# A diffusion backbone kernel: filler matmuls ahead of attention, late modulation columns moved to the first MLP, semaphore clears inside other stages

## What is computed

```python
for i in range(2):
    mod_l = silu(c) @ mod_w[i] + mod_b[i]
    sh_a, sc_a, gt_a, sh_m, sc_m, gt_m = split(mod_l, 6)
    hl = rms_norm(xl, norm_g[i, 0]) * (1 + sc_a) + sh_a
    yl = ab_mixer(hl, hc, ...) if i == 0 else conv_mixer(hl, ...)
    xl = xl + gt_a * rms_norm(yl, norm_g[i, 1])
    hm = rms_norm(xl, norm_g[i, 2]) * (1 + sc_m) + sh_m
    xl = xl + gt_m * rms_norm(square(relu(hm @ w1[i])) @ w2[i], norm_g[i, 3])
```

```python
s_loc = einsum('bqhgd,bkhd->bhgqk', qblk, kb) * scale      # 3 blocks of 128 keys, banded
s_ctx = einsum('bqhgd,bkhd->bhgqk', qblk, kc) * scale      # 256 context keys
p = softmax(concatenate([s_loc, s_ctx, s_sink], axis=-1))
out = p[..., :n_loc] @ vb + p[..., n_loc:n_loc + L] @ vc
```

## Time and profile before

| | us |
|---|---|
| median of three runs | 1872.45 |
| lowest and highest of them | 1869.65, 1876.17 |
| the profiled execution | 1864.61 |
| its span, first to last instruction | 1862.4 |
| TensorE busy | 1681.7 (90%) |
| VectorE, ScalarE, GpSimd busy | 721.1, 571.2, 860.4 |

### The profile page before, as it was taken

The page is one execution under the profiler, slowest core; times in us unless marked ns, Lnnn a source line. Parts: engine busy times, 40 slices in busy tenths (PEclk is TensorE's granted clock), DMA queues, the critical chain, the costliest instruction groups (busy, mean ns, idle before and its releaser), DMA issues. The chain is left out here.

```text
span 1862.4 us, 35642 instructions
## 1 busy us (share of the span) xinstructions
PE 1681.7 (90%) x15570; PEld 1379.0 (74%) x15570; DVE 721.1 (39%) x1060; ACT 571.2 (31%) x816; POOL 860.4 (46%) x399
## 2 busy tenths in 40 slices
PE   4899999976788889588999999999998999999996
PEld 2688778865667678366788888888886778888885
DVE  2332233337757675554212121461066431212134
ACT  3423233343343432223313232313222242313230
POOL 1433100008786763243687888763443244444441
PEclk9998955558999999787999999978998799999998
DMA  8211100002231222211344334421221112222221
GB/s 327 106 68 68 32 1 1 1 0 71 71 137 50 93 72 72 75 68 45 136 142 152 135 135 152 147 71 45 105 90 68 68 59 101 90 92 111 90 90 45
DMA packets 23618, 162.16 MB, mean 87 GB/s; under 512 B 2624, under 2 KB 3264, under 8 KB 4800
## 3 DMA queue, kind: packets, MB, share of 16 engines
q1 hardware_dynamic: 21904, 154.09, 23.1%
q10 hardware_dynamic: 1584, 6.13, 0.8%
HBM read 157.71 MB, written 2.10 MB: 86 GB/s over the span
## 5 line engine op out<-in xcount | busy, mean ns | idle before, releaser
L218 POOL TENSOR_TENSOR v<-raw,v 128x1024 fp32r<-128x1024 f32 x160 | 387.8, 2445 | 427.1 <-ACT v L206 401.0
L235 PE MATMUL bank<-hm,v 128*128 128x512 f32 x2112 | 487.5, 392 | 10.4 <-PEq L161 4.6
L235 PEld LDWEIGHTS bank<-hm,v 128*128 128x128 f32 x2112 | 398.5, 189 | 100.2 <-issue 12.7
L235 PE MATMUL bank<-hid,v 128*128 128x512 f32 x1536 | 349.5, 389 | 0.0
L235 PEld LDWEIGHTS bank<-hid,v 128*128 128x128 f32 x1536 | 288.4, 188 | 59.8
L206 ACT ACTIVATE v<-raw 128x2048 fp32r<-128x2048 f32 x77 | 147.5, 1916 | 421.0 <-PE bank L235 420.9
L1975 DVE TENSOR_TENSOR bank<-bank,rl 128x512 f32<-128x512 f32 x64 | 44.7, 699 | 277.4 <-ACT rl L1954 277.4
L218 POOL TENSOR_TENSOR w<-raw,w 128x1024 fp32r<-128x1024 f32 x22 | 54.1, 2481 | 137.2 <-ACT w L206 137.2
L949 POOL TENSOR_TENSOR kt<-kt,kk 128x768 f32<-128x768 f32 (+2 forms) x12 | 14.9, 1270 | 216.6 <-ACT kt L1263 216.6
L935 POOL TENSOR_TENSOR raw<-raw,cs 128x2048 f32<-128x2048 f32 x24 | 87.0, 3627 | 51.1 <-DVE at L1380 51.1
L512 PE MATMUL bank<-h,w 128*128 128x512 f32 x600 | 108.8, 343 | 0.0
(11 more groups left out here) (286 smaller groups left out, 2413.1 us busy)
## 6 DMA issues: line engine op xcount, KB each, us to landing
raw<-w_in SPq DMA_DIRECT2D x119, 1024.0 KB, 4.8
mraw<-wm_in SPq DMA_DIRECT2D x16, 1024.0 KB, 4.8
raw<-wm_in SPq DMA_DIRECT2D x3, 1024.0 KB, 15.8
xres<-x_in ACTq DMA_DIRECT2D x1, 2048.0 KB, 8.3
yb<-wm_in SPq DMA_DIRECT2D x2, 1024.0 KB, 19.2
mixed_in<-wm_in SPq DMA_DIRECT2D x2, 1024.0 KB, 23.1
xres<-x_in SPq DMA_DIRECT2D x1, 2048.0 KB, 7.3
out_T<-xres ACTq DMA_DIRECT2D x8, 256.0 KB, 2.0
```

The lines of the kernel that those rows point to most:

```text
L218: i = nc.gpsimd.tensor_tensor(W[1][n % 2][:, k:k + 4], raw[n % 2][:, k:k + 4], W[0][n % 2][:, k:k + 4].bitcast(F32), SUB)
L235: last = nc.tensor.matmul(bank(b(s, m), 0, hi - lo), W[w][s][:, k, m * P:(m + 1) * P], H[h][:, k, lo:hi], start=(k == 0 and w == h == 0), ...
```

## The change

It has three parts.

1. Four fillers stand behind the scores of units 0 and 1, and two ahead of each of units 1 and 2.
2. Twenty of the late columns stand at the end of the first MLP, behind a wait for `mprod_free` and ahead of `over_channels`. Twelve stay in the late norm: four in place of its first filler, six behind the first broadcast (`over_partitions`, L185), two behind the second. None stands between the token sums.
3. `clear` and `clear_then_block` are gone. Semaphores live longer: those of the first stages until the end of the RWKV stage, the RWKV stage's own until the end of the first MLP, all others to the program's end. `reset` clears the first list (59) on GpSimd at the start of the RWKV stage, and the second (47) on GpSimd at the start of the first MLP. The 66 others aren't cleared.

```diff
+    until_rwkv, until_mlp = ExitStack(), ExitStack()
+    signals = {until_rwkv: [], until_mlp: [], top: []}
+
     def sems(stack, *names):
-        return [stack.enter_context(nc.semaphore(own(n))) for n in names]
+
+        out = [stack.enter_context(nc.semaphore(own(n))) for n in names]
+        signals[stack] += out
+        return out
+
+    def reset(pool, stack):
+
+        for s in signals[stack]:
+            pool.sem_clear(s)
...
-    def clear(stack_sems):
-
-        with nc.Block() as block:
-            @block.gpsimd
-            def _(pool):
-                for s in stack_sems:
-                    pool.sem_clear(s)
...
-    def clear_then_block(stack_sems):
-        clear(stack_sems)
-        return nc.Block()
...
-        with clear_then_block(S) as block:
+        with nc.Block() as block:
...
                 scores(0)
                 scores(1)
+                keep_warm(4, bank(6))
                 for u in range(NU):
+                    if u in (1, 2):
+                        keep_warm(2, bank(7))
                     pe.wait_ge(exp_ready, 2 * u + 1)
...
+            reset(pool, until_rwkv)
             for p in range(PAIRS):
                 key_products(p)
...
-                        keep_warm(1, bank(5))
+                        late_columns(20, 24)
+                        if late is None:
+                            keep_warm(1, bank(5))
                         pe.wait_ge(inv_ready, 1)
                         over_partitions(pe, rcol[:, 0, :], bank(6)).then_inc(rst_done, 1)
-                        late_columns(0, 8)
+                        late_columns(24, 30)
...
-                            late_columns(8 + 2 * k, 10 + 2 * k)
-                        late_columns(24, 28)
...
-                        late_columns(28, 32)
+                        late_columns(30, 2 * LATE)
...
                     if late is not None:
+                        reset(pool, until_mlp)
                         pool.sem_inc(mprod_free, 1)
...
+                    if late is not None:
+                        pe.wait_ge(mprod_free, 11)
+                        for t in range(20):
+                            nc.tensor.matmul(bank(5, t, t + 1), late[:, t * P:(t + 1) * P], K("ones", 0, 1), start=True,
+                                             stop=True)
                     squares.over_channels(pe)
```

More of the change, by code:

```diff
@@ L276, in build @@
         early.append(early[1])
-        early_in = sems(st, *(f"early_in{n}" for n in range(EARLY)))
-        S = sems(st, "const_in", "x_in", "cst_in", "csig", "cs_ready", "eps_ready", "early_used", "rows_ready", "folded",
+        early_in = sems(until_rwkv, *(f"early_in{n}" for n in range(EARLY)))
+        S = sems(until_rwkv, "const_in", "x_in", "cst_in", "csig", "cs_ready", "eps_ready", "early_used", "rows_ready", "folded",
                  "mod_ready", "sq_ready", "sq_used", "acc_ready", "ssum_done", "total_ready", "root_ready", "inv_ready",
@@ L876, in build @@
              "dve_chain", "ones_ready", "pc_ready")
-    S = sems(drw, *names, "x_back")
+    S = sems(until_mlp, *names, "x_back")
     (lora_done, sig_ready, cum_ready, exp_ready, kp_ready, kpk_ready, bb_ready, prod_ready, at_ready, rt_ready,
@@ L1527, in _ @@
             state_output(PAIRS - 1)
+    until_rwkv.close()
     rw_sb.close()
@@ L1623, in __init__ @@
             self.sq, self.acc = sb(st, "ysq", [P, T]), sb(st, "yacc", [P, T])
-            self.ready, = sems(st, "ysum_ready")
-            clear([self.ready])
+            self.ready, = sems(top, "ysum_ready")
         def add(self, dve, t):
@@ L1868, in mlp @@
                 mprod = sb(st, "mprod", [P, KT, 256])
-                L = sems(st, "mraw_loaded", "mprod_free", "mprod_ready", "mprod_half", "mprod_quarter")
+                L = sems(top, "mraw_loaded", "mprod_free", "mprod_ready", "mprod_half", "mprod_quarter")
                 mraw_loaded, mprod_free, mprod_ready, mprod_half, mprod_quarter = L
-                clear(L)
             hid = [sb(st, f"hid{i}", [P, KT, T], F32R) for i in range(2)]
@@ L1874, in mlp @@
             sq = [bank(4), bank(5)]
-            S = sems(st, "relu_ready", "sq_ready", "hid_hi", "hid_ready")
+            S = sems(top, "relu_ready", "sq_ready", "hid_hi", "hid_ready")
             relu_ready, sq_ready, hid_hi, hid_ready = S
@@ L2012, in build @@
     mlp(S_MLP0, False, late)
+    until_mlp.close()
     norms(0, "g03", 40, "g10", 1, 0, S_CIN, late=late)
@@ L2019, in build @@
         u = sb(st, "u", [P, KT, T + 2])
-        S = sems(st, "c_ready", "chi_ready", "clo_ready", "conv_chain")
+        S = sems(top, "c_ready", "chi_ready", "clo_ready", "conv_chain")
         c_ready, chi_ready, clo_ready, conv_chain = S
@@ L2061, in projection @@
             pe_block(pe, S_COUT, W, hc, parts=one, ready=lambda k: (clo_ready, k + 1))
-        clear(S)
         dense(S_CIN, 12, lambda t: gates[:, t, :] if t < 2 * KT else None, W, h,
```

8 lines of the change are left out of this document (4 added, 4 removed).

## The result

| us | before | after | ratio (95%) |
|---|---|---|---|
| median, runs of the first comparison | 1871.05 (4) | 1767.68 (4) | 0.9449 (0.9423 to 0.9475) |
| lowest, highest | 1868.33, 1876.17 | 1766.91, 1771.78 | |
| the same kernels in a later comparison | 1865.00 (9) | 1771.71 (5) | 0.949 (0.9465 to 0.9515) |
| profiled execution, its span | 1864.61, 1862.4 | 1766.91, 1765.1 | |
| mean granted clock | 0.901 | 0.942 | |

The kernel is faster by 103 us in the one comparison and by 93 in the other. By the spans of these two profiled executions the gain is 97.3 us, where the sum had 89.3. Each kernel was profiled a second time (e1 with a span of 1867.7, e9 with 1773.4), and the four pairs give 89.0 to 102.6 us.

A forecast was written before the change was run, and what follows sets the result against it. TensorE at half clock was taken to bound attention. Savings of 72.3 (attention), 15.7 (clears) and 1.3 (columns), 89.3 in sum, took 1864.6 to 1775.3; 7.8 for the median gave 1783 us, range 1769 to 1812.

The forecast's parts named there:

- the sum: Whole kernel: attention 72.3, clears 15.7 and late columns 1.3 us saved, 89.3 in all, taking the profiled 1864.6 to 1775.3.
- The forecast 91.2: Attention stretch: from 163.5 to 91.2 us with fillers at the full clock, 72.3 us saved (bounds 54 and 76.6).
- the front fillers, priced at 2.6: Four fillers before the first transposes: delay of 2.6 us (1.5 to 5.1), the clock mostly falling in the gap before them.
- 85 was taken between 81.8 and 97: Attention stretch without fillers at full clock: floor 81.8 us, 97 if gaps between kinds of matmul stay; 85 taken.
- The rule on transposes: Attention units: the skill's rule that transposes aren't counted as clock activity, which would bring the first rival's 1868 us.
- Rivals 1 and 2: Attention: clock not held, 1868 us, chance 0.09; or another chain takes over or level lost midway, 1820 us, chance 0.09.
- 15.7 us: Clear stages: 172 semaphores at 0.07 us and 16 stages at 0.23, all engines standing still; 15.7 us saved (13 to 16.5).
- What is late next is in each case the first instruction of the following stage: Behind each clear stage: only the following stage's first instruction, which hung on the release, was late.
- rival 4: Stages' ends cost the same without clears, another wait being just as late: 15 us less saved, 1798; chance 0.04.
- The cover on GpSimd: RWKV stage and first MLP: 106 clears on GpSimd (4.1 and 3.3 us) stand ahead of products and delay nobody, or barely.
- 1.3 us was forecast: Late columns: 8 us off the late norm against 6.7 at the MLP's end; 1.3 saved (1.2 lost to 3.4 saved).
- The 7.8 us: Last step: the three-run median's distance above the profiled execution, added to 1775.3 to give the median forecast 1783 us.

The follow-up runs named there:

- e1: The kernel before, unchanged, profiled a second time: 1870.05 us, ratio 1.001.
- e9: The changed kernel once more, untouched, with a second profile: 1771.71 us.
- e6: The changed kernel with only the four front fillers, without the pairs ahead of units 1 and 2: 1766.85 us, ratio 0.9439.
- e10: The changed kernel without the pairs of fillers ahead of units 1 and 2, four in front kept, in a later comparison: 1765.29 us, ratio 0.9451.
- e13: The changed kernel with two fillers in front of the first transposes and none later: 1765.97 us, ratio 0.9446.
- e8: The changed kernel with a 256-column filler behind each of the first seven token sums of three norms: 1781.68 us, ratio 0.9543.
- e7: The changed kernel with 32 transposes of a constant in place of the four front fillers, later pairs kept: 1779.24 us, one run.
- e3: The kernel before with only the clear stages taken away, no fillers, late columns where they were: 1844.39 us, ratio 0.9871.
- e11: The changed kernel with only one filler in front of the first transposes and none later: 1843.97 us.
- e14: The changed kernel with no filler in front and four ahead of the transposes of unit 12: 1804.12 us.
- e2: The kernel before with the eight fillers alone, clear stages and late columns as before: 1801.62 us, ratio 0.9632.
- e4: The kernel before with only the late columns moved: 1872.08 us, ratio 1.0019.
- e12: The changed kernel with four fillers in front, none later, and all late columns back in the late norm: 1770.03 us.
- e5: The changed kernel with all late columns back in the late norm, fillers and clears' part kept: 1772.75 us, ratio 0.949.
- e15: The changed kernel with an empty stage at each of the 16 places of the former clears: 1783.72 us, ratio 0.9526.

## Why the prediction was right, and where it failed

**Attention: right in mechanism, and near in size.** The clock is 1.00 in all units, and a unit takes 2.83 us (2.6 to 2.9 forecast). From the first transposes to the output's it is 91.3 us (234.82 to 326.14). The forecast 91.2 had the front fillers in it, which stand ahead of this stretch and delay the first transposes by 1.0 us (4.60 from the first scores, 3.64 before). With them it is 92.3, and the saving 71.2 where 72.3 stood. Two of its terms were off in opposite directions. The units at full clock take 87.8 (91.3 less two pairs, 3.5), where 85 was taken between 81.8 and 97: a bit more of the gaps stays than was thought. And the front fillers, priced at 2.6, cost 1.0; e6 and e10 with four of them are 1.3 us longer than e13 with two. They were priced with a fall of the clock in the gap ahead of them. In the first profile it didn't fall, so they ran at full clock and fitted the wait; in e8 it fell while they ran. One term was missing: the sixteen transposes of the output also run at full clock, 1.97 us for 3.67, which is 1.7 more.

**The rule on transposes** spoke for 0.50 in the units. e7 and the units themselves, five of thirteen matmuls a transpose, say otherwise. Rivals 1 and 2 had the right worry with the wrong condition: e3, e11 and e14 show that the units do stay at 0.50 for as long as nothing dense comes, and e11 beside e13 that one filler more ahead of them, with 0.9 us less of wait, decides it.

**The clears: mis-sized, the smaller step that failed.** 15.7 us was a length, 172 times a clear and 16 times a stage, and as a length it was right: TensorE's gaps at the stages' starts and ahead of the last norm's broadcast are 15.8 us shorter in sum. But taking the clears away alone gave 21.8 us by medians (e3; 18 to 30 by the interval of its ratio). The failed step is "What is late next is in each case the first instruction of the following stage": that instruction isn't only later, it also mostly ran at half clock behind the gap, and the following ones with it. Beyond its shorter gap the first norm is 1.7 us shorter in e3 than before (41.68 to 38.20, 1.78 of it gap), and the late norm 3.2 (48.99 to 45.30, 0.54 of it gap); their first fillers went from 1.87 to 1.10 and from 2.04 to 1.10. The RWKV stage's first row went from 5.49 (e2) to 2.85. It isn't the same in each execution: in e9 the first norm starts at half clock, and the norm behind the convolution does so in both traces of the changed kernel (2.05, 1.90). And the changed kernel doesn't have the late norm's 3.2 us, since its columns at the MLP's end let the clock fall before. TensorE's gap ahead of the RWKV stage went from 4.60 to 1.51 us, 3.1 for 3.5 forecast, and rival 4 is refuted. The cover on GpSimd held.

**The late columns: near, by the rows.** 1.3 us was forecast. The columns and sums at the MLP's end take 4.52 + 1.59 + 1.85 us, of which the sums had taken some 2.5 before (1229.67 to 1232.24); 5.1 more, 6.7 forecast. The rows give 1.9 us in sum for the move alone (e4) and 0.5 beside the other parts (e12, e10). The medians give nothing that can be told for e4 and 4.7 for e12 and e10. Between 0 and 5 is open.

**From the sum to the median: the main step that failed.** "The median of the three runs is 7.8 us above the profiled one, so the forecast for a median is 1783." The 7.8 us were no cost around the span. They were one execution's place in a scatter of 5 to 10 us: the kernel before had medians from 1865.00 to 1871.05 over five comparisons, and the changed one had its profiled execution 0.8 below its median once and 4.5 above it once. The sum as it stood, 1775.3, is 3.6 us from the 1771.71 of e9 and 7.6 from 1767.68. Of the 15.4 us between the forecast (1783.1 before rounding) and the first median, 7.0 are this offset (7.8 added, 0.8 found) and 8.4 the sum, which was too small by that against the profiled 1766.91. The offset also lifted the range's low end, and with both it ended 1.3 us too high. The 8.4 us can't be told apart into clears and scatter: they would be 0.9 the other way by e9's profile (1776.22).

**What isn't settled.** By medians the parts alone give 64.5, 21.8 and -5.9, together 80 us, and the whole 93 to 103. Fillers and clears together (e5) give 96.7, where the two alone give 86.3. Of this 1.7 us is in the front fillers of the profiled executions (5.40, 3.70), but e8 shows that the 5.40 come without clear stages too. All of it lies within the three intervals, each some 6 us to a side. How often the clock falls in the front fillers of the changed kernel, and whether it is the filling of the wait or the amount of dense work that keeps it up, no run shows.

**A better version.** Two or four fillers in front and none later, with the rest of the change: 1765.97 (ratio 0.9446) and 1765.29 (0.9451), both below the changed kernel of e9 (0.949), though the intervals of these ratios overlap. Two rest on two executions, four on nine.

## What to carry to other kernels

A stretch in which TensorE is busy all the time can stay at half clock from end to end, because its own mix of work leaves the clock where it was. Look for a granted clock of 0.50 beside 100% busy, find the idle TensorE ahead of it, and fill that wait: here two 512-column float32 matmuls (1.98 us) in a wait of 2.1 us gave 77 us (171.6 from first scores to RWKV stage in e3, 94.6 in e13), one gave 2 (169.8), and the pairs behind cost their own length. Fillers in the middle of such a stretch work too (e14). Price a stage's end not only by its length but by what runs at half clock behind it. And don't carry the distance between one profiled execution and a median over to another kernel; put it into the range, on both sides.

## What the runs showed of the hardware

- The units' work holds either level of the clock for as long as it runs: 0.50 over 160 us (e3, e11), 1.00 over 92 us, both at 100% busy TensorE, and 4.66 us of fillers lead from one to the other (e14). The one change inside them without a filler is e11's fall, 2 us behind the end of its wait of 1.08 us.
- Float32 transposes hold the clock (e7, one execution: 3.71 us of them, 1.00 throughout).
- The same instructions behind the same gap don't meet the same clock in each execution: the four front fillers take 3.70 us in six traces and 5.40 in e8, the first norm's first filler 1.10 us in eleven and 1.96 in e9.
- 5.3 us of empty barriers took 8 to 18 us (e15); why more than their length isn't shown.
- A VectorE product of two SBUF operands that takes 0.69 us alone took 1.67 to 11.03 us beside GpSimd's subtractions. This, the place of the clock's falls and an unexplained 6 us in the RWKV stage are what the traces of one kernel differ by.
